# One long kernel, three places: who makes the high parts of a projection's weights, which column groups the first stage multiplies, and in which order latent attention begins

## The chip, the cores and the metric

The kernel runs on one core of one Trainium2 chip. The metric is the device time of one execution in microseconds, the median over several runs. A profiled execution gives the trace from which the rows below come.

## What is computed

The reference is two transformer blocks behind one another on x of 1024 tokens by 1024 features, batch 1, all in float32.

The first block normalizes x, makes six modulation vectors from one condition vector (`silu(c) @ w_ada + b_ada`, 1024 by 6144, split into shift, scale and gate twice), projects the modulated x by `w_in` into the inputs of a latent attention and of a retention mixer, mixes, projects back, and ends with a feed-forward part:

```python
mod = c_act @ w_ada[l] + b_ada[l]
sh1, sc1, gt1, sh2, sc2, gt2 = [m[:, None, :] for m in jnp.split(mod, 6, axis=-1)]
h = x * (1.0 + sc1) + sh1
proj = h @ w_in[l]
...
a = mla_mixer(...)            # 8 heads, causal, 64 plain + 32 rotated features per head
x = layer_norm(ALPHA * x + gt1 * y, ln1_g[l], ln1_b[l])
```

The second block has an "even" and an "odd" layer. The even layer projects 1024 features to 2560 (`e_w_in`), both for the 1024 tokens and for a context of 256, runs a depthwise convolution of 31 taps over 512 channels, and a Fourier mix over others.

## The kernel before

Activations lie with features on the 128 partitions: a tile is 128 features by 1024 tokens, eight tiles make a tensor (`X`, and `HH` and `HL` below). A large product is made of *units*: 128 output features for all tokens, accumulated in one PSUM tensor `G[s]` over eight feature tiles. To keep float32 accuracy with fast matrix products, activations and weights are both split into a rounded high part and the remainder: `HH` and `HL` for activations, `WH` and `WL` for weights; a unit is HH x WH, HL x WH and HH x WL (`gemm_unit`, line 304). For each unit SP loads a weight tile `RAW` (512 KB), POOL makes `WH` by a copy that rounds (line 266 or 278) and then `WL = RAW - WH` (line 269 or 281). Two buffers of each exist, so unit i can be split when unit i-2 has been multiplied (`unit_done`). Some engine then empties `G[s]` and increments `unit_freed`.

The program is a list of stages. In each, every engine has its own instruction list, and an engine enters a stage when ACT, PE and DVE have all left the one before (`gate`). POOL and SP run ahead, held only by their semaphores. TensorE alone may run the first unit of a following stage inside the one before (`lead_in`, the *lead unit*), as its activations appear.

- Stage `start`: SP loads x (eight DMAs) and then six column groups `ADA[g]` of `w_ada`, 512 columns each, 2 MB each: groups 0 and 1 are the shift, 2 and 3 the scale, 4 and 5 the gate of the first half. SP's queue then continues with the first weight tiles of `win`. TensorE multiplies groups 1 and 2 by the condition vector in products with one column (`ada`, line 506). DVE makes groups 0 and 3 by a multiplication (line 470) and a reduction (line 473), which TensorE sums over partitions (line 515). TensorE turns x (line 523), DVE writes tile f of `X` (line 481), ScalarE scales it with the modulation and makes `HH` (lines 420, 423), DVE makes `HL` (`h_low`, line 427). At the end TensorE multiplies groups 4 and 5.
- Stage `win`: 16 units of `w_in`. Beside it DVE makes the modulation vectors of the second half by rows (`Modulation`, block of 1024 columns: eight loads `WVEC` of 512 KB and eight multiply-adds, lines 374 and 377, then eight short sums on TensorE, line 393): three blocks. SP issues, at step j, the store of a tile of `X` to DRAM (6 <= j < 14), the weights of unit j, and two `WVEC` loads, in this order.
- Stage `mla` (latent attention): products of query and key parts (line 951, 959) and values (967); for the rows of a head's scores, eight maxima (`largest`, line 983, reduced by DVE, line 1245), which become a row of the query (`row`, `put_row`), then the steps of scores, exponential and values. The rotated 32 features are made by DVE (`rope_plain`, `rope_swapped`), rounded by ScalarE (`rope_high`, line 1126), completed by DVE (`rope_low`, line 1239) and put into the heads' tiles by SP's DMAs (line 1329).
- Stage `ein`: 20 units of `e_w_in`, each with the context's columns beside it (`side`, line 307). Units 0 to 7 feed the convolution, which DVE runs from SBUF to SBUF, tap by tap, for the 1024 tokens (`ACC`) and the 256 of the context (`ACCC`): four channel tiles of 31 taps, line 1945, in one streak of 88 taps from the moment unit 7 is done. At a change of channel tile there are two copies (line 1950) and two instructions with one input (line 1942). ScalarE empties the units 8 to 19. POOL splits all 20 by `split_unit`.

Of the kernel before, what the change touches and what calls it, by code (L numbers as in the profile page):

```python
# [14 lines left out]
F32 = mybir.dt.float32  # L15
# [7 lines left out]
P = 128  # L23
# [111 lines left out]
def build_program(nc, A, out):  # L135

    ctx = ExitStack()
    with ctx:
# [211 lines left out]
        class Modulation:  # L350
# [7 lines left out]

            def load(self, sp, q):
                g, (b, k) = self.first + q, divmod(q, KT)  # L360
                w, _, j, _, _ = self.blocks[b]
                need(sp, vec_used[g % 2], g // 2)
                sp.dma_start(self.raw[q % 2][:], A[w][k * P:(k + 1) * P, j * P:j * P + D]).then_inc(vec_loaded[g % 2], 16)

            def rows(self, dve, q):
                g, (b, k), raw = self.first + q, divmod(q, KT), self.raw[q % 2]
# [4 lines left out]
                for x, v in enumerate(xs):  # L371
                    acc = self.sums[b % 2][x][:]
                    if k == 0:
                        dve.tensor_scalar(acc, raw[:], v[:, 0:1], None, ALU.mult).then_inc(S("mod_row"), 1)
                    else:
                        dve.wait_ge(S("mod_row"), self.rows_done + 1 - len(xs))
                        dve.scalar_tensor_tensor(out=acc, in0=raw[:], scalar=v[:, k:k + 1], in1=acc, op0=ALU.mult,
# [7 lines left out]
            def sum(self, pe, b):  # L385
# [4 lines left out]
                for j in range(KT):  # L390
                    for x in range(len(xs)):
                        c = MOD_COL + j * len(xs) + x
                        m = pe.matmul(M[b % 2][:, c:c + 1], self.sums[b % 2][x][:, j * P:(j + 1) * P], ONES[:, 0:1],  # L393
                                      start=True, stop=True)
# [40 lines left out]
        ADA = [Z(f"ADA{g}", [P, KT, 512], F32, 64 + 16 * g if g < 4 else 32 + 16 * (g - 4)) for g in range(6)]  # L435

        def start_sp(sp, r0):
            for t in range(NT):
                sp.dma_start(XT[:, t, :], A["x"][t * P:(t + 1) * P, :]).then_inc(S("x_in"), 16)
            for g in range(6):  # L440
# [3 lines left out]
        def start_dve(dve):  # L444
# [20 lines left out]
            prod = X[:, 0:4, :].rearrange("p a (b n) -> p (a b) n", n=512)  # L465
            for i, g in enumerate((0, 3)):
                dve.wait_ge(S(f"ada{g}"), 16)
                if i:
                    dve.wait_ge(S("ada_rows"), 2)
                dve.tensor_tensor(prod, ADA[g][:], CACT[:].unsqueeze(2).broadcast_to([P, KT, 512]), ALU.mult)\  # L470
                   .then_inc(S("ada_rows"), 1)
                dve.wait_ge(S("ada_rows"), 2 * i + 1)
                dve.tensor_reduce(X[:, 4 + i, 0:512], prod.rearrange("p k n -> p n k"), AX.X, ALU.add)\
                   .then_inc(S("ada_rows"), 1)
# [4 lines left out]
            for f in range(KT):  # L479
                dve.wait_ge(S("li_tr"), f + 1)  # L480
                dve.tensor_scalar(X[:, f, :], M[f % 2][:], vec("ln_in_g", f), vec("ln_in_b", f), ALU.mult,
                                  ALU.add).then_inc(S("li_x"), 1)
                if f:
                    h_low(dve, "li", f - 1, SEQ)
            h_low(dve, "li", KT - 1, SEQ)
            dve.wait_ge(S("ada_sum"), 6)
            dve.tensor_tensor(MODA[:, 16:24], G[1][:, 0:8], vec("b_ada", 16, 8), ALU.add).then_inc(S("mod_in"), 1)
# [11 lines left out]
        def start_pe(pe):  # L499
            def ada(g):  # L500

                pe.wait_ge(S(f"ada{g}"), 16)
                for u in range(4):
                    col = 4 * (g % 4) + u
                    for k in range(KT):
                        m = pe.matmul(G[g // 4][:, col:col + 1], ADA[g][:, k, u * P:(u + 1) * P], CACT[:, k:k + 1],  # L506
                                      start=(k == 0), stop=(k == KT - 1))
                m.then_inc(S("ada_sum"), 1)
            pe.wait_ge(S("c_act"), 2)
            for g in (1, 2):  # L510
                ada(g)
            for i, g in enumerate((0, 3)):
                pe.wait_ge(S("ada_rows"), 2 * i + 2)
                for u in range(4):
# [2223 lines left out]
```

## Time and profile before

| what | value |
|---|---|
| median of 3 runs | 2986.7 us (2984.83 to 2994.78) |
| profiled execution | 2987.89 us |
| its span, first to last instruction | 2986.1 us |
| PE busy | 2587.2 us (87%) |
| DVE busy | 1375.1 us (46%) |
| POOL busy | 835.1 us (28%) |
| ACT busy | 569.2 us (19%) |

Busy time counts an instruction from its start to its end, including time in which it waits for a port inside. The shares are averages over stages that have different limits, so each edit has to be judged in its own stage. Of ends of TensorE's instructions the profile has only a model.

### The profile page before, as it was taken

How to read it: one execution, taken by the hardware profiler on the slowest of the kernel's cores; microseconds unless marked ns; L12 is line 12 of the kernel's file. 1: busy time of each engine (PE TensorE's matmuls, PEld its weight loads, DVE VectorE, ACT ScalarE, POOL GpSimd, SP SyncE). 2: the span in 40 equal slices, each digit the busy share in tenths (PEclk: the TensorE clock that was granted, in tenths of full speed). 3: DMA queues.
4: the chain of work that ended last, by engine and by line, in shares of the span. 5: the costliest groups of instructions: out<-in, count | busy, mean ns of one | idle time of the engine just before them, and what ended most of it. 6: DMA issues, size and time to landing. Idle time of an engine off the chain costs nothing.

```text
span 2986.1 us, 29208 instructions
## 1 busy us (share of the span) xinstructions
PE 2587.2 (87%) x11738; PEld 2026.1 (68%) x11738; DVE 1375.1 (46%) x1554; ACT 569.2 (19%) x818; POOL 835.1 (28%) x505
## 2 busy tenths in 40 slices
PE   5999668899999999999994994699498799959998
PEld 5887345567678888888762783575276588838877
DVE  7261753334643444444447689603523313046643
ACT  2001123440432101111125200000202300013310
POOL 1132230005463233223452358610021233210011
PEclk9799868999999999999997997899798899979999
DMA  7252000013132232222222100011211111140001
GB/s 259 92 169 64 18 16 0 15 57 96 56 102 85 88 99 89 78 88 85 80 86 92 36 28 16 28 32 44 86 52 33 36 49 42 42 104 16 1 15 71
DMA packets 219710, 190.12 MB, mean 64 GB/s; under 512 B 14928, under 2 KB 193744, under 8 KB 219344
## 3 DMA queue, kind: packets, MB, share of 16 engines
q1 hardware_dynamic: 214144, 167.93, 18.8%
q0 software_dynamic: 3872, 14.93, 1.3%
q10 hardware_dynamic: 1584, 5.77, 0.5%
q8 instruction: 72, 1.18, 0.2%
q14 instruction: 38, 0.31, 0.0%
HBM read 167.76 MB, written 13.63 MB: 61 GB/s over the span
## 4 chain that ended last, share of the span: by engine, by line
PE 72%; DVE 12%; issue 6%; ACT 4%; PEld 2%; DMA 1%; POOL 1%; PEldq 1%; SPq 1%; ACTq 0%; DVEq 0%; POOLq 0%
PE G L304 26%; PE G L1573 25%; PE M L2496 3%; PE M L307 2%; PE G L1029 2%; DVE WPT L2532 2%; PE M L2481 1%; PE M L1588 1%; PE M L393 1%; PE G L2060 1%; PE M L2060 1%; PEld G L506 1%; PE M L983 1%; PE M L951 1%; PE G L2191 1%
## 5 line engine op out<-in xcount | busy, mean ns | idle before, releaser
L304 PE MATMUL G<-HH,WH 128*128 128x512 f32 x1264 | 406.7, 402 | 118.7 <-POOL WL L269 71.9
L304 PE MATMUL G<-HL,WH 128*128 128x512 f32 x1264 | 401.2, 398 | 0.0
L304 PE MATMUL G<-HH,WL 128*128 128x512 f32 x1264 | 400.7, 397 | 0.0
L266 POOL TENSOR_SCALAR WH<-RAW 128x1024 fp32r<-128x1024 f32 x64 | 189.8, 2966 | 745.0 <-PE G L304 458.0
L278 POOL TENSOR_SCALAR WH<-RAW 128x1024 fp32r<-128x1024 f32 (+1 forms) x152 | 129.9, 855 | 929.0 <-PE G L1573 508.8
L304 PEld LDWEIGHTS G<-HH,WH 128*128 128x128 f32 x1264 | 224.6, 191 | 174.3 <-issue 115.7
L281 POOL TENSOR_TENSOR WL<-RAW,WH 128x1024 fp32r<-128x1024 f32 (+1 forms) x152 | 294.4, 1937 | 12.7
L304 PEld LDWEIGHTS G<-HL,WH 128*128 128x128 f32 x1264 | 225.6, 191 | 47.3
L304 PEld LDWEIGHTS G<-HH,WL 128*128 128x128 f32 x1264 | 225.4, 191 | 47.5
L1573 PE MATMUL G<-HH,WH 128*128 128x512 f32 x640 | 228.4, 405 | 14.2 <-POOL WL L281 9.5
L1573 PE MATMUL G<-HL,WH 128*128 128x512 f32 x640 | 225.0, 400 | 0.0
L1573 PE MATMUL G<-HH,WL 128*128 128x512 f32 x640 | 224.9, 400 | 0.0
L1704 DVE SCALAR_TENSOR_TENSOR X<-G,MODA,X 128x512 f32<-128x512 f32 (+1 forms) x96 | 97.4, 1015 | 206.5 <-PE G L1573 206.2
L1573 PE MATMUL G<-FHT,WH 128*128 128x512 f32 x512 | 177.1, 407 | 8.9 <-issue 5.3
L1720 DVE TENSOR_TENSOR FLT<-T,FHT 128x1024 fp32r<-128x1024 f32 (+1 forms) x40 | 53.3, 1332 | 278.9 <-ACT FHT L1661 278.9
L1573 PE MATMUL G<-FLT,WH 128*128 128x512 f32 x512 | 174.5, 402 | 0.0
L1573 PE MATMUL G<-FHT,WL 128*128 128x512 f32 x512 | 173.7, 400 | 0.0
L1945 DVE SCALAR_TENSOR_TENSOR ACC<-U,V,ACC 128x1024 f32<-128x1024 f32 x120 | 162.5, 1354 | 0.7 <-DVE UC L1965 0.7
L269 POOL TENSOR_TENSOR WL<-RAW,WH 128x1024 fp32r<-128x1024 f32 x64 | 160.0, 2500 | 5.3
L1573 PEld LDWEIGHTS G<-HH,WH 128*128 128x128 f32 x640 | 122.1, 191 | 48.1 <-issue 11.9
L1657 ACT ACTIVATE T<-G 128x1024 f32<-128x1024 f32 (+1 forms) x40 | 34.2, 855 | 604.3 <-PE G L1573 604.3
L1573 PEld LDWEIGHTS G<-HL,WH 128*128 128x128 f32 x640 | 121.8, 190 | 31.0 <-issue 1.7
(467 smaller groups left out, 4097.7 us busy)
## 6 DMA issues: line engine op xcount, KB each, us to landing
RAW<-in_w_ff SPq DMA_DIRECT2D x40, 512.0 KB, 4.0
RAW<-in_w_ff SPq DMA_DIRECT2D x80, 256.0 KB, 2.8
ADA<-in_w_ada SPq DMA_DIRECT2D x6, 2048.0 KB, 19.7
WVEC<-in_w_ada SPq DMA_DIRECT2D x24, 512.0 KB, 4.5
FVEC<-in_e_w_mod SPq DMA_DIRECT2D x24, 512.0 KB, 4.0
FVEC<-in_o_w_mod SPq DMA_DIRECT2D x24, 512.0 KB, 3.9
RAW<-in_o_w_in SPq DMA_DIRECT2D x24, 512.0 KB, 3.7
RAW<-in_e_w_in SPq DMA_DIRECT2D x20, 512.0 KB, 3.7
```

The lines of the kernel that those rows point to most:

```text
L266: pool.tensor_scalar(WH[s][:], RAW[s][:], 1.0, 0.0, ALU.mult, ALU.add).then_inc(w_high, 1)
L269: pool.tensor_tensor(WL[s][:], RAW[s][:], WH[s][:].bitcast(F32), ALU.subtract).then_inc(w_split[s], 1)
L278: pool.tensor_scalar(hi, raw, 1.0, 0.0, ALU.mult, ALU.add).then_inc(w_high, 1)
L281: pool.tensor_tensor(lo, raw, hi.bitcast(F32), ALU.subtract).then_inc(w_split[U % 2], 1)
L304: m = pe.matmul(G[s][:, n * w:(n + 1) * w], part[s][:, k, :], acts[i][:, k, n * w:(n + 1) * w], start=first, stop=last)
L307: m = pe.matmul(M[s][:, 0:CTX], part[s][:, k, :], side[i][:, k, :], start=first, stop=last)
L1029: pe.matmul(G[1][:, cols_], VP[:, kb_, first:first + P], PF[g % 4][:, 0:n], start=(kb_ == 0), stop=(kb_ == 4 * c + 3)).then_inc(S("ml_pv"), 1)
L1573: m = pe.matmul(G[s][:, half(h)], part[s][:, k, :], moving[:, half(h)], start=(j == 0 and part is WH and moving is hi), stop=(j == len(ord ...
L1704: dve.scalar_tensor_tensor(out=X[:, f, cc], in0=G[U % 2][:, cc], scalar=gate, in1=X[:, f, cc], op0=ALU.mult, op1=ALU.add).then_inc(unit_fr ...
L1945: dve.scalar_tensor_tensor(out=acc[:], in0=u[:, j, k:k + T], scalar=wk, in1=acc[:], op0=ALU.mult, op1=ALU.add).then_inc(tap, 1)
L2060: m = pe.matmul(dst, vv[:, tt, g * P:(g + 1) * P], tab[:, q * half:(q + 1) * half], start=(i == 0 and q == 0), stop=(q == 1 and (t >= NT o ...
L2496: m = pe.matmul(M[1][:, c0:c0 + HEAD], WPT[i % 2][:, b * P:(b + 1) * P], v, start=(b == 0), stop=(b == len(blocks) + 1))
```

## The change

1. In stage `ein`, `WH` of units 2 to 19 is made by ScalarE (`ein_high`), after it has emptied unit i-2; POOL has its own program there, waits for ScalarE's copy and makes only `WL`. Units 0 and 1 are split as before.
2. In stage `start`, groups 4 and 5 are neither loaded nor multiplied. Group 1 alone is multiplied by TensorE; groups 2 and 3 are made by DVE by rows (one multiplication and seven multiply-adds of 512 columns each), group 0 by POOL by rows (eight multiplications and seven additions). TensorE turns two tiles ahead of the sums, and DVE writes these two tiles of `X` before it adds up the modulation. The gate is a fourth block of `Modulation` in `win`, with buffers in `X`, whose tiles are therefore stored from step 2 on.
3. In stage `mla`, ScalarE rounds the rotated part of the first query pair first; its high parts go out by two DMAs with a semaphore of their own, and the first maxima wait for these alone. `v_part(0)` moves behind the first maximum, the maxima of head 0 alternate between two PSUM tensors, `scores(0)` comes after the fifth of them and `row(0, 0)` after the first two scores. ScalarE loads the exponential's table at the stage's begin. POOL makes the key rows of heads 1 to 3 only after DVE's `rope_low(0)`.

```diff
-        ADA = [Z(f"ADA{g}", [P, KT, 512], F32, 64 + 16 * g if g < 4 else 32 + 16 * (g - 4)) for g in range(6)]
+        ADA = [Z(f"ADA{g}", [P, KT, 512], F32, 64 + 16 * g) for g in range(4)]
+        ROWS = {g: X[:, 4 + i, 0:512] for i, g in enumerate((2, 3, 0))}
...
-            for i, g in enumerate((0, 3)):
+            for i, g in enumerate((2, 3)):
                 dve.wait_ge(S(f"ada{g}"), 16)
...
+                dve.tensor_scalar(ROWS[g], ADA[g][:, 0, :], CACT[:, 0:1], None, ALU.mult).then_inc(S("ada_rows"), 1)
+                for k in range(1, KT):
+                    dve.wait_ge(S("ada_rows"), KT * i + k)
+                    dve.scalar_tensor_tensor(out=ROWS[g], in0=ADA[g][:, k, :], scalar=CACT[:, k:k + 1], in1=ROWS[g],
+                                             op0=ALU.mult, op1=ALU.add).then_inc(S("ada_rows"), 1)
...
+        def start_pool(pool):
+            part = X[:, 7, 0:512]
+            pool.wait_ge(S("c_act"), 2)
+            pool.wait_ge(S("ada0"), 16)
+            pool.tensor_scalar(ROWS[0], ADA[0][:, 0, :], CACT[:, 0:1], None, ALU.mult).then_inc(S("ada_pool"), 1)
+            for k in range(1, KT):
+                pool.wait_ge(S("ada_pool"), 2 * k - 1)
+                pool.tensor_scalar(part, ADA[0][:, k, :], CACT[:, k:k + 1], None, ALU.mult).then_inc(S("ada_pool"), 1)
+                pool.wait_ge(S("ada_pool"), 2 * k)
+                pool.tensor_tensor(ROWS[0], ROWS[0], part, ALU.add).then_inc(S("ada_pool"), 1)
...
+            pe.wait_ge(S("li_xn"), NT)
+            for f in range(2):
+                turn(f)
+            pe.wait_ge(S("ada_pool"), 2 * KT - 1)
+            sums(0)
+            for i, g in enumerate((2, 3)):
+                pe.wait_ge(S("ada_rows"), KT * i + KT)
+                sums(g)
+            for f in range(2, KT):
+                turn(f)
...
-        WMOD = Modulation([ada_block(j) for j in (24, 32, 40)], [Z("WVEC0", [P, D], F32, 72), Z("WVEC1", [P, D], F32, 60)],
-                          [[Z("WSUM0", [P, D], F32, 56)], [Z("WSUM1", [P, D], F32, 52)]])
+        WMOD = Modulation([ada_block(j) for j in (24, 32, 40, 16)],
+                          [Z("WVEC0", [P, D], F32, 72)[:], Z("WVEC1", [P, D], F32, 60)[:], X[:, 1, :], X[:, 2, :]],
+                          [[Z("WSUM0", [P, D], F32, 56)[:]], [Z("WSUM1", [P, D], F32, 52)[:]], None, [X[:, 0, :]]])
...
+            WMOD.sum(pe, 3)
...
-                if 6 <= j < 14:
-                    sp.dma_start(SPILL[:, j - 6, :], X[:, j - 6, :]).then_inc(x_spilled, 16)
+                if 2 <= j < 10:
+                    sp.dma_start(SPILL[:, j - 2, :], X[:, j - 2, :]).then_inc(x_spilled, 16)
                 if j >= 4:
                     load_unit(sp, (r0 + j) // 2, j % 2, win_unit(j), RAW[j % 2][:])
-                if j < 12:
-                    WMOD.load(sp, 2 * j)
-                    WMOD.load(sp, 2 * j + 1)
+                if j == 12:
+                    sp.wait_ge(x_spilled, 16 * KT)
+                WMOD.load(sp, 2 * j)
+                WMOD.load(sp, 2 * j + 1)
...
-                need(pe, S("ml_mx"), 8 * h + n)
+                ps = M[0]
+                if h == 0:
+                    need(pe, S("ml_mx"), n - 1)
+                    if n % 2:
+                        pe.wait_ge(S("ml_qlo"), 2)
+                        ps = G[0][:, 512:] if n > 4 else G[0]
+                else:
+                    need(pe, S("ml_mx"), 8 * h + n)
...
-            v_part(0)
             pe.wait_ge(S("ml_rot"), 2)
             for n in range(NT):
                 largest(0, n)
+                if n == 0:
+                    v_part(0)
                 if n == 4:
                     row(0, 1)
-            row(0, 0)
-            scores(0)
+                    scores(0)
...
+            act.wait_ge(mla_split, N_SPLIT)
+            act.activation(PF[0][0:1, 0:32], IDENT[0:1, 0:32], ACT.Exp)
+            rope_high(0)
             q_high(0)
             k_high(0)
-            rope_high(0)
...
+            sp.wait_ge(S("ml_qrh"), 1)
+            for odd in range(2):
+                put(0, odd, 0, S("ml_rope_first"))
+            sp.wait_ge(S("ml_qr"), 1)
+            for odd in range(2):
+                put(0, odd, 1, S("ml_rope_in0"))
...
+        def ein_high(act, i):
+
+            r, U_ = info("ein")["r0"] + i, info("ein")["u0"] + i
+            if 2 <= i < 20:
+                act.wait_ge(raw_loaded[r % 2], (r // 2) * 16 + 16)
+                act.wait_ge(unit_done[U_ % 2], U_ // 2)
+                act.activation(WH[U_ % 2][:], RAW[r % 2][:], ACT.Copy).then_inc(ein_wh, 1)
+
+        def ein_pool(pool):
...
+                if i < 2:
+                    split_one(pool, r, U_, KT)
+                    continue
+                pool.wait_ge(ein_wh, i - 1)
+                pool.sem_inc(w_high, 1)
+                pool.wait_ge(w_split[U_ % 2], U_ // 2)
+                pool.tensor_tensor(WL[U_ % 2][:], RAW[r % 2][:], WH[U_ % 2][:].bitcast(F32), ALU.subtract)\
+                    .then_inc(w_split[U_ % 2], 1)
```

## Rows read from the trace of the kernel before

**Rows 1.** Stretches: length, busy us (instructions) by engine, PE clock, DMA share, GB/s.

```profile
75.00:102.00 27.00, 27.00 (x128) 27.00 (x128) 5.30 (x5) 4.93 (x5) 0.00 (x0) 0.50 0.00 1
...
116.00:290.00 174.00, 173.33 (x767) 140.09 (x768) 73.19 (x72) 4.36 (x4) 53.76 (x28) 1.00 0.45 136
...
1826.00:1862.00 36.00, 13.48 (x71) 11.22 (x69) 35.90 (x47) 3.48 (x5) 35.92 (x2) 0.76 0.00 0
```

**Rows 2.** Timeline of PE, first stage: start us, us, line, names, [idle before]

```profile
25.59 27.44 PE L506 MATMUL G<-CACT,ADA 128*128 128x1 f32 x128 [25.59 <-DMA ADA<-in_w_ada]
...
52.89 1.85 PE L515 MATMUL G<-ONES,X 128*128 128x1 f32 x8
...
57.42 6.26 PE L523 MATMUL M<-IDENT,XT 128*128 128x128 f32 x32
...
116.08 0.71 PE L304 MATMUL G<-HH,WH 128*128 128x512 f32 x2 [0.36 <-PEq L2638]
```

**Rows 3.** Timeline of DVE, first stage

```profile
26.53 5.88 DVE L462 TENSOR_SCALAR XT<-XT,MV,RS 128x1024 f32<-128x1024 f32 x8
...
32.31 4.42 DVE L470 TENSOR_TENSOR X<-ADA,CACT 128x4096 f32<-128x4096 f32 x1
...
59.41 1.34 DVE L481 TENSOR_SCALAR X<-M,V 128x1024 f32<-128x1024 f32 x1 [1.43 <-PE M L523]
```

**Rows 4.** Timeline of ACT, first stage

```profile
60.85 1.24 ACT L420 ACTIVATE T<-X,MODA 128x1024 f32<-128x1024 f32 x1 [34.59 <-DVE X L481]
...
62.13 1.06 ACT L423 ACTIVATE HH<-T 128x1024 fp32r<-128x1024 f32 x1
```

**Rows 5.** Timeline of DVE, stage win

```profile
128.89 3.41 DVE L377 SCALAR_TENSOR_TENSOR WSUM<-WVEC,CACT,WSUM 128x1024 f32<-128x1024 f32 x1 [1.61 <-DMA WVEC<-in_w_ada]
...
133.58 1.28 DVE L377 SCALAR_TENSOR_TENSOR WSUM<-WVEC,CACT,WSUM 128x1024 f32<-128x1024 f32 x1
...
167.08 2.14 DVE L564 SCALAR_TENSOR_TENSOR ANGR<-TURN,ANGR 128x512 f32<-128x512 f32 x3
```

**Rows 6.** Timeline of POOL, stage win

```profile
128.82 2.40 POOL L281 TENSOR_TENSOR WL<-RAW,WH 128x1024 fp32r<-128x1024 f32 x1
```

**Rows 7.** Timeline of POOL, stage ein

```profile
1661.96 1.05 POOL L266 TENSOR_SCALAR WH<-RAW 128x1024 fp32r<-128x1024 f32 x1 [17.62 <-PE M L307]
...
1690.40 8.90 POOL L266 TENSOR_SCALAR WH<-RAW 128x1024 fp32r<-128x1024 f32 x1 [10.39 <-PE M L307]
...
1718.24 9.52 POOL L266 TENSOR_SCALAR WH<-RAW 128x1024 fp32r<-128x1024 f32 x1 [10.39 <-PE M L307]
...
1773.92 32.60 POOL L266 TENSOR_SCALAR WH<-RAW 128x1024 fp32r<-128x1024 f32 x1 [10.38 <-PE M L307]
...
1809.58 1.93 POOL L266 TENSOR_SCALAR WH<-RAW 128x1024 fp32r<-128x1024 f32 x1 [0.32 <-POOL WL L269]
...
1880.78 36.24 POOL L266 TENSOR_SCALAR WH<-RAW 128x1024 fp32r<-128x1024 f32 x1 [11.52 <-PE M L307]
```

**Rows 8.** Timeline of DVE, stage ein

```profile
1761.65 2.97 DVE L1945 SCALAR_TENSOR_TENSOR ACC<-U,V,ACC 128x1024 f32<-128x1024 f32 x1 [0.24 <-DVE UC L1965]
...
1772.90 1.28 DVE L1945 SCALAR_TENSOR_TENSOR ACC<-U,V,ACC 128x1024 f32<-128x1024 f32 x1
...
1774.49 1.28 DVE L1945 SCALAR_TENSOR_TENSOR ACC<-U,V,ACC 128x1024 f32<-128x1024 f32 x1
...
1810.53 1.25 DVE L1945 SCALAR_TENSOR_TENSOR ACCC<-UC,V,ACCC 128x256 f32<-128x256 f32 x1
```

**Rows 9.** Chain that ended last, latent attention's begin

```profile
437.82 0.95 ACT QRH L1126
...
444.62 1.19 PE M L983 x2
...
463.57 3.77 PE M L951 x12
```

**Rows 10.** Chain that ended last, in stage win

```profile
161.12 1.68 PE M L393 x16
```

More of the change, by code:

```diff
@@ L357, in __init__, with raw_of, sums_of @@
                 vec_count[0] += KT * len(blocks)
+            def raw_of(self, q):
+                return self.raw[q % 2 + (2 if len(self.raw) == 4 and q >= 3 * KT else 0)]
+            def sums_of(self, b):
+                return self.sums[b if b < len(self.sums) and self.sums[b] else b % 2]
             def load(self, sp, q):
@@ L392, in sum @@
                         c = MOD_COL + j * len(xs) + x
[L393 removed]
+                        m = pe.matmul(M[b % 2][:, c:c + 1], self.sums_of(b)[x][:, j * P:(j + 1) * P], ONES[:, 0:1],
                                       start=True, stop=True)
@@ L439, in start_sp @@
                 sp.dma_start(XT[:, t, :], A["x"][t * P:(t + 1) * P, :]).then_inc(S("x_in"), 16)
-            for g in range(6):
+            for g in range(4):
                 sp.dma_start(ADA[g][:], A["w_ada"][:, 512 * g:512 * g + 512].rearrange("(k p) n -> p k n", p=P))\
@@ L499, in start_pe, with sums, turn @@
         def start_pe(pe):
-            def ada(g):
-                pe.wait_ge(S(f"ada{g}"), 16)
+            def sums(g):
                 for u in range(4):
[L504 to L514, printed above, removed]
-                    m = pe.matmul(G[0][:, 4 * g + u:4 * g + u + 1], X[:, 4 + i, u * P:(u + 1) * P], ONES[:, 0:1],
+                    m = pe.matmul(G[0][:, 4 * g + u:4 * g + u + 1], ROWS[g][:, u * P:(u + 1) * P], ONES[:, 0:1],
                                   start=True, stop=True)
                 m.then_inc(S("ada_sum"), 1)
-            pe.wait_ge(S("li_xn"), NT)
-            for f in range(KT):
+            def turn(f):
                 if f >= 2:
@@ L573, in win_dve @@
             for j in range(16):
+                for q in (2 * j, 2 * j + 1):
+                    WMOD.rows(dve, q)
                 if j < 12:
-                    for q in (2 * j, 2 * j + 1):
-                        WMOD.rows(dve, q)
                     unit_ready(dve, u0 + j)
@@ L1046, in extras @@
                     if i == 0:
+                        row(0, 0)
+                    if i == 1:
                         take()
@@ L1093, in mla_pe, with rope_rows @@
             spread(N_PAIR - 1)
+        def rope_rows(pe, h, high):
+            j = h // 2
+            if j == 0:
+                pe.wait_ge(*((S("ml_rope_first"), 32) if high else (S("ml_rope_in0"), 32)))
+            else:
+                pe.wait_ge(S(f"ml_rope_in{j % 2}"), (0, 64, 96, 128)[j])
         def ROW_AT(h):
@@ L1171, in extras @@
                     chunk(h - 1, 0)
+                if h == 0 and i == 0:
+                    put_row(0, 0)
                 if h == 0 and i == 4:
@@ L1972, in ein_dve @@
             conv(dve, step, 4 * CONV_W)
+        ein_wh = whole("ein_high")
+        def ein_high(act, i):
[5 more added lines that the diff above has]
+        def ein_pool(pool):
+            r0, u0 = info("ein")["r0"], info("ein")["u0"]
+            for i in range(20):
+                r, U_ = r0 + i, u0 + i
+                if i < 2:
[6 more added lines that the diff above has]
+                    .then_inc(w_split[U_ % 2], 1)
+                pool.wait_ge(w_split[U_ % 2], U_ // 2 + 1)
+                pool.sem_inc(raw_used[r % 2], 1)
         def ein_act(act):
@@ L1995, in ein_act @@
                 act.sem_inc(unit_freed[U_ % 2], 1)
+                ein_high(act, 10 + j)
         def ein_src(j):
             return A["e_w_in"][:, ein_cols[j]:ein_cols[j] + P].rearrange("(k p) n -> p k n", p=P)
-        stage("ein", dict(lead=lead_in("ein", SEQ, "en_lo", side=(HHC, HLC)), act=ein_act, dve=ein_dve,
+        stage("ein", dict(lead=lead_in("ein", SEQ, "en_lo", side=(HHC, HLC)), act=ein_act, dve=ein_dve, pool=ein_pool,
                           pe=lambda pe: gemm_pairs(pe, info("ein")["u0"], 10, SEQ, (HH, HL), led=True, side=(HHC, HLC))),
```

94 lines of the change are left out of this document (51 added, 43 removed).

## The prediction

> **What bounds the kernel now.** I began with the granted clock and busy time by stretch, because a share of the span hides that the three edited places have different limits. Four stretches matter [rows 1]. From 75 to 102 us TensorE does 128 instructions for gate columns and nothing else, at half clock, with every other engine nearly idle: it is the bound. From 116 to 290 TensorE is busy 173.3 of 174 us: that stage (`win`) hides whatever DVE, POOL and the queues do, so long as its weights arrive. From 1826 to 1862 TensorE is busy 13.5 of 36 us, while POOL is "busy" 35.9 in two instructions: POOL is the bound, and behind POOL something else. The timelines of the engines then say what.
>
> In the first stage, TensorE makes the products of column groups 1 and 2 from 25.59 to 53.0, sums DVE's rows for groups 0 and 3, and turns tiles; after the last turn it makes groups 4 and 5, and only then, at 102, starts the lead unit of `win`, which lasts until 115.7 (the next unit's first row, 116.08, less its 0.36 of idle time), when `win` proper begins [rows 1, 2]. DVE scales x from 26.53 to 32.3 and works on rows for groups 0 and 3 from 32.31 until about 55.6, the turns of 57.42 less the last sum's 1.85 [rows 2, 3]. ScalarE's first tile of h begins at 60.85, 1.24 for the scaled tile and 1.06 for its high part, so one tile per 2.3 us [rows 4].
>
> In `ein` a POOL copy WH<-RAW, 1.05 us at 1661.96, takes 8.9, 9.5 and then three times over 32 us (first and last of the three in [rows 7]). Its starts show the pace of a unit: 1690.40 to 1718.24 is two units, so 13.92 us each. DVE meanwhile runs the convolution, a tap of x and a tap of the context every 1.59 us, each instruction starting before the one ahead has ended [rows 8]. POOL gets in only when DVE pauses or changes channel. Once in, it gets in again: at 1809.58 the next copy waits for one DVE instruction (1.93 us), and then DVE is the one that is stretched (1.25 us for a 256-column tap) [rows 7, 8].
>
> **Start, products of the gate removed.** Groups 4 and 5 cost 27.0 us on the path [rows 1]. They go to `win` as eight more DVE rows and 8 column sums.
>
> **Start, products of groups 0, 2, 3 by rows.** TensorE keeps group 1 alone: its data lands at 25.59, half of the 27.4 us is 13.7, so it ends at 39.3. Two turns (the 32 transposes took 6.26, so about 1.6 to 1.9 each) end at 43.0, three sums of 1.85 at 48.6 [rows 2]. On DVE, a 512-column multiply-add is 2.14/3 = 0.71 us with its wait [rows 5]; two groups are 2 x (0.45 + 7 x 0.71) = 10.9 us, instead of 23.3. From 32.3 [rows 3] that ends at R = 43.5 if nothing disturbs it (R is when DVE's rows are done). POOL's group 0 is 8 multiplications and 7 additions of 512 columns; at half the 1.05 of a copy [rows 7] and half the 2.4 of a subtraction [rows 6], with some 0.1 us between, 8 x 0.63 + 7 x 1.3 = 14 us, from about 20 us (group 0 lies 2 MB ahead of group 1 in the same queue, which moves about 370 GB/s there).
>
> But POOL and DVE exclude each other: a DVE multiply-add that started at 128.89 beside POOL's subtraction of 128.82 took 3.41 us instead of 1.28: it ended 1.1 us after POOL's, which had taken 2.40 [rows 5, 6]. They do not share, one waits for all of the other. About 7 us of POOL's row work lie after 26.5, and the splits of units 0 and 1 (two times 1.05 + 2.4 = 6.9 us), whose loads come 4 MB earlier than before, fall near 39. If all of this pushes DVE, R is 43.5 + 13.5 = 57.0. I take R = 54, near the exclusive end, since the row shows full exclusion, less some overlap with waits. Two tiles of x (1.34 each) follow R [rows 3], so the scale of h is ready at R + 2.7 = 56.7.
>
> From there to the end of the lead unit: turn 7 needs tile 5 of x, about 10 us after h begins, then 2 for the turn, then 13.7 for the unit, which starts at half clock as it did before, 102 to 115.7 [rows 1, 2]: 26 us in all. h itself comes at 2.3 per tile [rows 4], ahead of that. End 56.7 + 26 = 82.7 against 115.7: **-33**. Bounds: R = 43.5 (then the sums, 48.6, decide) ends at 74.6, -41; R = 57 ends at 85.7, -30.
>
> **`win`.** DVE's eight rows more, 1.28 us each [rows 5], find room: it works 73 of 174 us [rows 1]. Eight more loads of 0.5 MB pass SP, and the stores of X start at j = 2 instead of 6, ahead of the load of unit 4 with three stores instead of none. At 136 GB/s with 0.45 of the engines busy a full queue moves about 300 GB/s [rows 1], 1.7 us a store, so unit 4's weights can be 0 to 5 us late; there was some 3 us of room. I take 1. The fourth sum comes after the last unit: 1.68 us on TensorE [rows 10], less the 1.0 that ScalarE needs for its last tile anyway, plus two short DVE instructions behind it: 1. **+2**, bounds 0 and +5. SP's wait for all stores at j = 12 costs nothing: the last store is issued at j = 9.
>
> **Latent attention's begin.** Before, ScalarE copied the high parts of q and k until 437.82, then rounded the rotated part (0.95); DVE's low part, four of SP's DMAs and their landing followed, and the first maximum began at 444.62 [rows 9]. After, ScalarE rounds first, and only two DMAs of high parts stand before the maximum, in flight while q and k are copied. What is last is then the copy of k: 437.82 + 0.95 = 438.8 if everything on ScalarE moves back by the rounding. So -5.8 there. POOL's other key rows wait, so they no longer lie over DVE's addition. v_part (24 short products on TensorE) moves behind the first maximum, where DVE reduces; with two buffers the maxima overlap. Eight maxima, one behind the other, took from 444.62 to some 459, and DVE's eight reductions are 6 us of that; with TensorE's half under them I estimate 438.8 + 13.4 = 452.2 for scores(1) and 457.3 for q_part, one more step (1.3 us) then being done ahead of it, against 463.57 [rows 9]: 463.57 - 457.3 + 1.3 = 7.6, **-7.5**. Lower bound on the gain 4 (the begin alone, minus clock that falls in a new pause), upper 10. The exponential's table load leaves a place where it was covered; nothing.
>
> **`ein`, WH by ScalarE.** Removed from POOL: 18 copies. ScalarE gains 18 x 1.06 us [rows 4] in a stage where it is idle for 12 us of each 13.92; it makes WH(i) after it emptied unit i-2, 1.5 us later than POOL did, and TensorE has a unit's time for it. No cost. The question is who waits for DVE now. The subtraction WL stays on POOL and reads SBUF too; it is now POOL's *first* instruction after ten idle microseconds, in the place of the copy. The trace has no subtraction in that place: each follows its copy by 0.1 us. Its wait is between nothing and what the copy waited. The nearest rows are the copies, which never got in in mid-streak after idling (five of the six that came then, the sixth waited 1.3 us for a change of channel [rows 7]) and the one exclusion of a subtraction [rows 5, 6]; so I take the same wait. Then each channel change still lets through two units, and the gain is the copy and its intrusion into DVE, two changes of channel at 1 to 1.5 us and the last 1.05: **-4**, bounds -2 and -8.
>
> SBUF — State Buffer, section "Who interferes with whom", of the Trainium skill says that the second to issue is blocked until the first finishes. By that rule a copy waits at most 1.3 us; the 32.60 us in [rows 7] disagree, so the rule holds for one pair and not for a streak. Were it to hold for the subtraction, `ein` would lose its stalls: rival 1.
>
> Sum: -33 + 2 - 7.5 - 4 = -42.5 on the profiled execution's 2987.9 (span 2986.1, 1.8 around it) gives 2945.4; the median of the runs shown is 1.2 lower, so 2944.
>
> **Rivals.** (1) The subtraction gets in between two taps, as it does after its copy. TensorE then runs through: the lead unit ends at 1661.9, so unit 14 starts 13 x 13.92 later, at 1842.9. It started when the copy of 1880.78 and its subtraction were done, at 1919.5: 76.6 later, and each stall also cost about 1 us of half clock. DVE takes 88 taps of 1.59 from 1761.7, 4 us of copies and 11 subtractions of 2.4, to 1932 [rows 7, 8], 6 us past TensorE's last unit (1661.9 + 19 x 13.92 = 1926). So -74 in place of -4: 2874. For it: after 1809.58 this happens, and the subtraction is another program on POOL. Against: the copies that waited. (2) It gets in at some places (a pause of the streak that now falls elsewhere): each of three stalls is worth some 22 to 25 us: 2895 to 2920. (3) The first stage gives less: POOL's row for group 0 is starved by DVE's eight scalings in a row (5.88 us [rows 3]) and by its rows, so the sum of group 0 comes last, R at 62: -25, total 2952 to 2960. (4) The other side: `win` becomes load-bound. Loads of weights stand behind two rows and a store on SP, and if they lag each unit from 4 to 15 by over 3.5 us, 12 x 3.5 = 42 us eat the whole gain; 5 us each would give 3004. Against: TensorE waited under 1 of 174 us, and the extra stores only move. (5) No net change, by half of that.
>
> **Chances.** Forecast 0.58 (its own range, bounds of the four terms added: -59 to -31, so 2928 to 2956); rival 1 0.20; rival 2 0.10; rival 3 0.07; rival 4 0.03; rival 5 0.02. The range reaches from rival 1 with a margin of 5 to the forecast's slow end: 2868 to 2957. 0.3% is 9 us, about what a measurement here tells from no change: faster 0.95, same 0.02, slower 0.03.
>
> **What would show it.** After: `win` proper begins near 83 us; DVE rows of 512 end near 54 and some are stretched to about 1.9 us; TensorE in `win` is busy all but 2 us. The first maximum of head 0 comes 16 us after TensorE's first product of the stage, not 22. In `ein`, WL rows of 30 us and more stand where WH rows stood, three times, with TensorE at 13.5 busy in 36. The prediction is wrong if those WL rows are 2.4 to 3.7 us long, if R is past 60, or if TensorE waits for unit 4.

## The result, and the profile after

| kernel | median of runs | profiled run |
|---|---|---|
| before, beside it | 2986.47 us (2984.83 to 2994.78, 4 runs) | 2987.89 us |
| changed | 2941.27 us (2934.71 to 2952.76, 4 runs) | 2934.71 us |

The ratio is 0.9847, 95% interval 0.9812 to 0.9883: 45 us faster, in the middle of the forecast's range and 3 us from its number. The profiled run of the changed kernel is the fastest of its four, so its trace shows 53 us. The kernel before has a median of 2979.38 us in 23 runs told below, 7 us less than in the four beside the changed kernel, so the gain may well be nearer to 37 than to 45 us. Of all runs told below, one execution of the last version (4267.05 us, mean granted clock 0.553 where its others had 0.943) is left out of its ratio.

Where the 53 us lie, by the starts of the same instructions in both traces:

| stretch | before | changed | difference |
|---|---|---|---|
| start of the program to the end of the lead unit of `win` | 115.7 | 83.8 | -31.9 |
| `win` | 175.9 | 177.6 | +1.7 |
| retention's products ahead of latent attention (code unchanged) | 73.9 | 66.5 | -7.4 |
| latent attention's first product to its first maximum | 22.0 | 16.0 | -6.0 |
| from there to its last division | 225.8 | 224.7 | -1.1 |
| output projection and feed-forward (unchanged) | 946.9 | 942.5 | -4.4 |
| `ein`, from the end of unit 8 to the last unit emptied | 232.5 | 228.7 | -3.8 |
| all the rest (unchanged) | | | about -0.3 |

The four edited places make 41 us; the forecast's terms for them were -33, +2, -7.5 and -4, which is -42.5. The other 12 us come from code that is the same, and some 3.5 us of the first row are not the edit's either, but the clock's (see the account of the start below).

Windows of the changed kernel (columns as in [rows 1]):

```profile
70.00:72.00 2.00, 1.43 (x7) 1.04 (x6) 2.00 (x3) 1.97 (x3) 0.00 (x0) 0.50 0.00 0
72.00:74.00 2.00, 2.00 (x12) 1.73 (x11) 2.00 (x3) 1.97 (x3) 0.00 (x0) 0.95 0.00 0
...
84.00:255.00 171.00, 169.72 (x750) 136.90 (x751) 83.60 (x79) 4.37 (x4) 54.15 (x28) 1.00 0.53 163
1774.00:1812.00 38.00, 14.03 (x73) 11.68 (x72) 37.90 (x47) 6.00 (x7) 35.07 (x1) 0.74 0.00 0
```

`win` is as full as before: TensorE waits 1.3 of 171 us, with the DMA share at 0.53 in place of 0.45. The last line is the stall of [rows 1] again: TensorE busy 14 of 38 us, POOL "busy" 35 in one instruction.

First stage, timeline of PE, then of DVE, then of POOL, of the changed kernel:

```profile
26.26 13.79 PE L536 MATMUL G<-CACT,ADA 128*128 128x1 f32 x64 [26.26 <-DMA ADA<-in_w_ada]
39.91 3.65 PE L530 MATMUL M<-IDENT,XT 128*128 128x128 f32 x16
46.70 3.58 PE L522 MATMUL G<-ONES,X 128*128 128x1 f32 x16 [3.14 <-POOL X L507]
58.51 1.86 PE L522 MATMUL G<-ONES,X 128*128 128x1 f32 x8 [8.24 <-DVE X L479]
...
72.39 0.71 PE L304 MATMUL G<-HH,WH 128*128 128x512 f32 x2
...
84.20 0.70 PE L304 MATMUL G<-HH,WH 128*128 128x512 f32 x2 [0.36 <-PEq L2727]
```

```profile
27.18 10.49 DVE L471 TENSOR_SCALAR XT<-XT,MV,RS 128x1024 f32<-128x1024 f32 x8
37.59 0.82 DVE L476 TENSOR_SCALAR X<-ADA,CACT 128x512 f32<-128x512 f32 x1
38.45 8.74 DVE L479 SCALAR_TENSOR_TENSOR X<-ADA,CACT,X 128x512 f32<-128x512 f32 x7
...
48.41 10.05 DVE L479 SCALAR_TENSOR_TENSOR X<-ADA,CACT,X 128x512 f32<-128x512 f32 x7
58.38 2.59 DVE L484 TENSOR_SCALAR X<-M,V 128x1024 f32<-128x1024 f32 x2
```

```profile
20.89 1.57 POOL L502 TENSOR_SCALAR X<-ADA,CACT 128x512 f32<-128x512 f32 x1 [17.82 <-DMA ADA<-in_w_ada]
...
45.16 1.49 POOL L507 TENSOR_TENSOR X<-X 128x512 f32<-128x512 f32 x1
46.62 1.48 POOL L278 TENSOR_SCALAR WH<-RAW 128x1024 fp32r<-128x1024 f32 x1
...
52.12 2.65 POOL L281 TENSOR_TENSOR WL<-RAW,WH 128x1024 fp32r<-128x1024 f32 x1
```

TensorE's third sum waits for DVE (8.24 us of idle time), so DVE's rows are what comes last. They end at R = 58.46. While POOL works, eight scalings take 10.49 us (5.88 in [rows 3]) and seven multiply-adds 8.74 and 10.05. The lead unit runs from 72.39 to 83.8, 11.5 us: the granted clock was 0.50 (1.2 GHz) only from 68.8 to 72.2 us, under the last turns, and back at its upper level (2.4 GHz) with the unit's first products.

Latent attention's begin, timeline of PE, and of ScalarE, changed kernel:

```profile
400.50 1.19 PE L1018 MATMUL M<-KHT,QHT 96*128 96x512 f32 x2 [3.79 <-ACT KHT L1150]
...
401.58 5.36 PE L994 MATMUL M<-WVV,KVS 128*128 128x128 f32 x24
```

```profile
395.18 1.06 ACT L1174 ACTIVATE QRH<-QROT 128x1024 fp32r<-128x1024 f32 x1 [9.26 <-DVE QROT L1287]
396.15 2.05 ACT L1150 ACTIVATE QHT<-G 64x1024 fp32r<-64x1024 f32 x2
398.22 2.06 ACT L1150 ACTIVATE KHT<-G 64x1024 fp32r<-64x1024 f32 x2
```

Rounding comes first, the copies of q and k hide the two DMAs, the maximum waits for k's copy alone.

`ein`, timeline of POOL, changed kernel:

```profile
1699.06 2.41 POOL L2055 TENSOR_TENSOR WL<-RAW,WH 128x1024 fp32r<-128x1024 f32 x1 [12.93 <-ACT WH L2043]
...
1726.96 31.29 POOL L2055 TENSOR_TENSOR WL<-RAW,WH 128x1024 fp32r<-128x1024 f32 x1 [12.98 <-ACT WH L2043]
1758.52 2.51 POOL L2055 TENSOR_TENSOR WL<-RAW,WH 128x1024 fp32r<-128x1024 f32 x1 [0.27 <-POOL WL L2055]
1776.86 35.07 POOL L2055 TENSOR_TENSOR WL<-RAW,WH 128x1024 fp32r<-128x1024 f32 x1 [15.83 <-ACT WH L2043]
1812.21 2.51 POOL L2055 TENSOR_TENSOR WL<-RAW,WH 128x1024 fp32r<-128x1024 f32 x1 [0.28 <-POOL WL L2055]
1830.98 34.65 POOL L2055 TENSOR_TENSOR WL<-RAW,WH 128x1024 fp32r<-128x1024 f32 x1 [16.26 <-ACT WH L2043]
```

Three subtractions of 31 to 35 us stand where three copies stood [rows 7], each followed by one that gets in at once.

### The profile page after: what moved, and what is told of

Read it like the earlier page. It is cut to its first block, busy times and chain, and to the rows that moved or that the text cites. A ratio compares the mean times of both kernels' runs of the same rounds, so it can differ in the third digit from the quotient of the medians.

```text
span 2932.9 us, 28884 instructions
## 1 busy us (share of the span) xinstructions
PE 2538.7 (87%) x11570; PEld 1980.0 (68%) x11570; DVE 1384.4 (47%) x1574; ACT 588.2 (20%) x837; POOL 825.4 (28%) x502
## 4 chain that ended last, share of the span: by engine, by line
PE 73%; DVE 12%; POOL 4%; ACT 4%; issue 3%; PEld 1%; DMA 1%; PEldq 1%; SPq 1%; ACTq 0%; DVEq 0%; POOLq 0%
PE G L304 26%; PE G L1634 25%; POOL WL L2055 3%; PE M L2585 3%; PE M L307 2%; PE G L1067 2%; DVE WPT L2621 2%; PE M L2570 1%; PE M L1649 1%; PE M L400 1%; PE G L2149 1%; PE M L2149 1%; PE M L978 1%; PE G L2280 1%; DVE HL L434 1%
## 5 line engine op out<-in xcount | busy, mean ns | idle before, releaser
L278 POOL TENSOR_SCALAR WH<-RAW 128x1024 fp32r<-128x1024 f32 (+1 forms) x154 | 136.1, 884 | 846.0 <-PE G L1634 501.6
L1634 PE MATMUL G<-HH,WH 128*128 128x512 f32 x640 | 227.6, 404 | 13.8 <-POOL WL L281 9.1
L266 POOL TENSOR_SCALAR WH<-RAW 128x1024 fp32r<-128x1024 f32 x44 | 46.6, 1060 | 593.0 <-PE G L304 457.2
L2055 POOL TENSOR_TENSOR WL<-RAW,WH 128x1024 fp32r<-128x1024 f32 x18 | 148.4, 8247 | 186.0 <-ACT WH L2043 185.2
```

Source lines behind the costliest of these rows:

```text
L278: pool.tensor_scalar(hi, raw, 1.0, 0.0, ALU.mult, ALU.add).then_inc(w_high, 1)
L1634: m = pe.matmul(G[s][:, half(h)], part[s][:, k, :], moving[:, half(h)], start=(j == 0 and part is WH and moving is hi), stop=(j == len(ord ...
L2055: pool.tensor_tensor(WL[U_ % 2][:], RAW[r % 2][:], WH[U_ % 2][:].bitcast(F32), ALU.subtract)\
```

## The experiments

**The parts one by one.** Each is the kernel before with one numbered part of the change, and one run is the changed kernel again, all on one chip (before there: 2979.38 us, 2968.33 to 2995.28, 23 runs).

Part 1 alone:

```diff
+                ein_high(act, 2 * j + 2)
+                ein_high(act, 2 * j + 3)
...
-        stage("ein", dict(lead=lead_in("ein", SEQ, "en_lo", side=(HHC, HLC)), act=ein_act, dve=ein_dve,
+        stage("ein", dict(lead=lead_in("ein", SEQ, "en_lo", side=(HHC, HLC)), act=ein_act, dve=ein_dve, pool=ein_pool,
```

> The kernel before with part 1 alone (WH of the even projection by ScalarE). Theory (the subtraction waits as the copy did): -4 us, 2982 to 2984, three WL of 31 to 36 us in the stage ein. Rival (the subtraction gets in between two taps): -70 or more, 2915, no WL above 4 us. In the trace of the changed kernel the stage ended 3.9 us earlier against its begin, but nothing there separates it from the clock.

2976.35 us (12 runs), ratio 1.0 (0.9979 to 1.0021): not told from no change. In the trace the stretch of `ein` is 227.8 us instead of 232.5, -4.7, and the three long waits are subtractions.

Part 2 alone:

```diff
-            for i, g in enumerate((0, 3)):
+            for i, g in enumerate((2, 3)):
...
+        def start_pool(pool):
...
-        WMOD = Modulation([ada_block(j) for j in (24, 32, 40)], [Z("WVEC0", [P, D], F32, 72), Z("WVEC1", [P, D], F32, 60)],
+        WMOD = Modulation([ada_block(j) for j in (24, 32, 40, 16)],
```

> The kernel before with part 2 alone (first stage without the gate's products, gate in win). Theory: the lead unit of win ends near 84 instead of 115.7 and win gives back 2: -30 us, 2956. Rival (part 2 also earned the 7 us by which the retention stage was shorter after, through something it moves): -37, 2949, and the retention stage shorter in every execution of it.

2946.62 us (6 runs), ratio 0.9895 (0.9869 to 0.9921), -33. The rival (that the shorter retention stretch belongs to this part) falls: that stretch is 66.3 us here, but also 66.3 and 66.5 in the runs of parts 1 and 3, whose first stage is the old one.

Part 3 alone:

```diff
+            rope_high(0)
             q_high(0)
             k_high(0)
-            rope_high(0)
...
+                if n == 0:
+                    v_part(0)
```

> The kernel before with part 3 alone (latent attention's begin). Theory: -7 us, 2979 to 2980, first maximum 16 us after the first product of the stage. Rival (the gain is lost again by the clock, which falls in the new pauses): 0 to -3.

2972.77 us (11 runs), ratio 0.9974 (0.9956 to 0.9992), -6.6; first product to first maximum 16.0 us, to the end 224.7, as in the whole change.

The changed kernel once more:

> The changed kernel once more. Theory of the clock: its profile differs from the one on record by several us in stages that the change does not touch (the retention stage 0 or 7 us longer, the feed-forward stage by 1.6 us steps), and the median comes out at 2941 to 2946, the sum of the three parts (-41 to -42). Rival: the 12 us in untouched stages belong to the change; then the profile repeats the one on record within 1 us per stage and the median is below 2938.

2942.29 us (4 runs), ratio 0.9884 (0.9858 to 0.9910), -37. The three parts add up to -42.4; the two measurements of the whole gave -45 and -37. Of the 8 us between these two, 7.1 lie in the kernel before (2986.47 and 2979.38) and 1.0 in the changed one. The sum and both measurements agree within their intervals, so no part is seen to work through another; with intervals of 8 us each way, an effect of a few us would not show. The retention stretch is 66.7 us in this profile too, so the theory's case of 7 us more did not come up.

**The wait of POOL in the convolution.** Prediction and change left the largest loss of `ein` in place, so it was tried next, on the changed kernel: one more wait for DVE on its own previous instruction, the context's tap. It orders nothing that was not in order already; it only makes the next tap of x start after the tap before it has ended.

```diff
                     if q:
                         dve.wait_ge(tap, q)
+                    if i == 0 and q:
+                        dve.wait_ge(S("ein_ctap"), q)
```

> The changed kernel, and in the convolution every tap of x also waits for the context's tap just ahead of it, so that DVE stops for a moment once per tap. Theory (POOL never gets in while DVE's instructions follow one another without a pause): WL enters at the next pause, no WL above 4 us, TensorE runs through, the stage ein about 70 us shorter, DVE's convolution its bound: 2870 to 2885. Rival (whatever DVE does, a POOL instruction after long idle time loses to two-input instructions): WL still 30 us and more, time 2941 to 2955.

2872.29 us (5 runs), ratio 0.9640 (0.9626 to 0.9655; before on this chip 2978.95 us, 11 runs). All subtractions take 2.4 to 3.5 us, and `ein` from the end of unit 8 to the last unit emptied is 154.9 us instead of 228.7. The price: a pair of taps every 1.79 us instead of 1.59, so the convolution ends 14 us after ScalarE has emptied the last unit. Hence the same at every eighth tap only:

```diff
+                    if i == 0 and q and q % 8 == 0:
+                        dve.wait_ge(S("ein_ctap"), q)
```

> As gap_each, but the additional wait stands at every eighth tap only. Theory: WL waits up to 8 taps, 13 us at most, mean 6 us; TensorE has 13.9 us per unit less 1.5 for ScalarE's emptying, 1.06 for its copy and 2.4 for WL, so about 9 us of wait are covered: nearly as fast as gap_each, within 10 us of it. Rival: as there, no gain.

2868.00 us (5 runs), ratio 0.9626 (0.9605 to 0.9648); the convolution now ends with the last unit. A window of this kernel, then POOL's timeline, then DVE's:

```profile
1774.00:1812.00 38.00, 38.00 (x199) 32.33 (x198) 37.69 (x39) 8.37 (x10) 9.16 (x3) 1.00 0.13 39
```

```profile
1736.58 8.47 POOL L2057 TENSOR_TENSOR WL<-RAW,WH 128x1024 fp32r<-128x1024 f32 x1 [12.98 <-ACT WH L2045]
1750.44 2.74 POOL L2057 TENSOR_TENSOR WL<-RAW,WH 128x1024 fp32r<-128x1024 f32 x1 [5.39 <-ACT WH L2045]
1764.37 2.69 POOL L2057 TENSOR_TENSOR WL<-RAW,WH 128x1024 fp32r<-128x1024 f32 x1 [11.19 <-ACT WH L2045]
```

```profile
1759.35 0.48 DVE L2008 SCALAR_TENSOR_TENSOR ACCC<-UC,V,ACCC 128x256 f32<-128x256 f32 x1
1759.93 1.28 DVE L2008 SCALAR_TENSOR_TENSOR ACC<-U,V,ACC 128x1024 f32<-128x1024 f32 x1
...
1764.32 0.47 DVE L2008 SCALAR_TENSOR_TENSOR ACCC<-UC,V,ACCC 128x256 f32<-128x256 f32 x1
1764.72 3.42 DVE L2008 SCALAR_TENSOR_TENSOR ACC<-U,V,ACC 128x1024 f32<-128x1024 f32 x1
```

TensorE is busy 38 of 38 us, at full clock. The pause is the 0.10 us between 1759.83 (1759.35 + 0.48) and 1759.93. But the subtraction of 1764.37 got in with no pause beside it: the next tap, 1764.72, is the one that waited (3.42 us). The one of 1736.58 had to wait 6 us, for the pause at 1742.8. What differs is the distance from the last pause.

**Does it need ScalarE's copies?** The kernel before, with the wait at every eighth tap alone:

```diff
+                    if i == 0 and q and q % 8 == 0:
+                        dve.wait_ge(S("ein_ctap"), q)
```

> The kernel before, with the one added wait of the experiment gap_8 in its convolution (every eighth tap of x also waits for the context's tap ahead of it); GpSimd still makes both parts of each weight tile. Theory (the pause is what lets GpSimd in, whoever makes the high parts): the copies WH<-RAW fall from over 30 us to under 9, TensorE waits for splits no longer, and the stage from its first split to its last unit's copy out is some 75 us shorter, as in gap_8: 2978 - 75 = 2903. Rival (the pause only works with ScalarE's copies, because a copy and a subtraction are two entries between taps and the copy is the harder one): at least two copies stay above 20 us and the time is 2925 or more.

2906.86 us (5 runs), ratio 0.9754 (0.9729 to 0.9779), -75, expected 2903; before on this chip 2981.51 us. POOL's timeline:

```profile
1786.23 1.85 POOL L266 TENSOR_SCALAR WH<-RAW 128x1024 fp32r<-128x1024 f32 x1 [9.89 <-PE M L307]
1788.16 2.46 POOL L269 TENSOR_TENSOR WL<-RAW,WH 128x1024 fp32r<-128x1024 f32 x1
...
1828.23 6.32 POOL L266 TENSOR_SCALAR WH<-RAW 128x1024 fp32r<-128x1024 f32 x1 [6.03 <-PE M L307]
```

The longest copy is 6.32 us and `ein` again 154.9: this one wait does nearly all, part 1 is not needed for it. Part 1 gets a use of its own only then: without it the convolution takes 162.3 us from the end of unit 8 on, with it (gap_8) 154.2, since DVE has ten copies fewer to let in there; it is the last to end.

**Distance of the pauses.** In twelve traces up to here, each GpSimd instruction that came while taps were running was set against the number of taps of x begun since DVE's last pause (a gap of 0.1 us, a channel change, a wait for a unit). Up to four: it waited 1.3 us or less. Five and more: until the next pause. The number of taps divides them better than the time does: in gap_8 the subtraction of 1750.44 came four taps, but 7.5 us, after a pause and waited 0.3 us, while that of 1736.58 came five taps and only 6.6 us after one and waited 6.1. Two runs to test this, as gap_8 with 4 and with 16 in the place of 8:

```diff
-                    if i == 0 and q and q % 8 == 0:
+                    if i == 0 and q and q % 4 == 0:
                         dve.wait_ge(S("ein_ctap"), q)
```

> The changed kernel with the added wait in the convolution at every fourth tap of x instead of every eighth. In the traces so far every GpSimd instruction that arrived at most four taps of x after the last pause in VectorE's streak (a gap between two of its instructions, however short) waited 1.3 us or less, also without a pause beside it, and those that arrived five to twelve taps after it waited for the next pause. If the number of taps since the last pause decides, no subtraction of the stage is over 3.8 us here (2.4 plus at most 1.3), where gap_8 still had four of 5.3 to 8.5. TensorE did not wait for those four, so the time is that of gap_8, 2868 plus or minus 8. Rival (what counts is that a pause happens to fall where GpSimd arrives): waits stay spread up to the distance of the pauses, 4 x 1.6 = 6.4 us, so subtractions of up to 8.8 us.

> The same with the added wait at every sixteenth tap of x (pauses also at the changes of channel, every 31 taps). By the taps since the last pause: subtractions that arrive within four taps of one take 2.4 to 3.7 us, those that arrive later take what is left to the next pause, up to 11 x 1.6 = 18 us and 2.4 more; GpSimd has some 11 us of room in each unit, so TensorE waits for the longest ones, by up to 9 us each, and the stage is 5 to 30 us longer than in gap_8, 2873 to 2898. No subtraction lasts over 21 us. Rival (one pause early in the streak is enough, what locks GpSimd out is something that builds up only over twenty taps and more): all under 4 us and the time of gap_8.

pause_4: 2865.54 us (4 runs), ratio 0.9620 (0.9573 to 0.9667), longest subtraction 3.54 us. pause_16: 2866.45 us (4 runs), ratio 0.9623 (0.9576 to 0.9670). POOL's timeline of pause_16:

```profile
1769.81 3.23 POOL L2057 TENSOR_TENSOR WL<-RAW,WH 128x1024 fp32r<-128x1024 f32 x1 [6.06 <-ACT WH L2045]
1783.73 12.52 POOL L2057 TENSOR_TENSOR WL<-RAW,WH 128x1024 fp32r<-128x1024 f32 x1 [10.69 <-ACT WH L2045]
1797.65 2.40 POOL L2057 TENSOR_TENSOR WL<-RAW,WH 128x1024 fp32r<-128x1024 f32 x1 [1.40 <-ACT WH L2045]
...
1841.16 15.03 POOL L2057 TENSOR_TENSOR WL<-RAW,WH 128x1024 fp32r<-128x1024 f32 x1 [11.35 <-ACT WH L2045]
```

These four came 3, 10, 2 and 9 taps after a pause. The second waited 10.1 us with the next pause 10.4 away, the fourth 12.6 with it 12.9 away. Over all fourteen traces: 104 instructions within four taps, longest wait 1.15 us; 65 beyond, every one waited until the streak's next break. The rivals of both runs fall. The time of pause_16 was missed: the stretch of `ein` is 161.5 us, 7.5 longer than in gap_8, inside the 5 to 30 us expected, but the median (2873 to 2898 expected) is that of gap_8. A difference of 7.5 us is within these intervals of 14 us each way, so this run doesn't show what the longer waits cost in all.

**The first stage.** DVE's rows came last, so POOL's work was taken from under them: first the splits of units 0 and 1, on the changed kernel.

```diff
                 pool.tensor_tensor(ROWS[0], ROWS[0], part, ALU.add).then_inc(S("ada_pool"), 1)
+            pool.wait_ge(S("ada_rows"), 2 * KT)
```

> The changed kernel, and POOL begins to split the weights of units 0 and 1 of win only when DVE's rows of groups 2 and 3 are done. Theory (POOL and DVE exclude each other, each us of POOL under DVE's rows costs DVE one): rows done at 51 to 52 instead of 58.5, the lead unit ends at 77 instead of 83.9, time -7. Rival (DVE's rows are slow for another reason, their data or their chain): rows still at 58, time 0.

2939.14 us (6 runs), ratio 0.9871 (0.9849 to 0.9893): no difference from the changed kernel that these runs can tell, where 7 us were expected. Then also POOL's rows of group 0 (the first half of the shift is left out, zeros stand in its place):

```diff
-            pool.tensor_scalar(ROWS[0], ADA[0][:, 0, :], CACT[:, 0:1], None, ALU.mult).then_inc(S("ada_pool"), 1)
...
-                pool.tensor_tensor(ROWS[0], ROWS[0], part, ALU.add).then_inc(S("ada_pool"), 1)
+            pool.memset(ROWS[0], 0.0).then_inc(S("ada_pool"), 2 * KT - 1)
```

> late_split with POOL's row for group 0 replaced by a memset: eight multiplications and seven additions are left out, and half of the shift is wrong by it. Theory of exclusion: DVE's eight scalings take 5.9 us again, not 10.5, and its rows 11 us; rows done at 44 to 45, the sums (48.6) then decide, lead unit ends near 75. Rival: scalings and rows as slow as in the changed kernel.

2938.57 us in a single run, whose profile has 7.3 us more in the retention stretch and 6.8 more in the feed-forward than the changed kernel's, so only its first stage is read here. DVE's timeline of late_split, then of no_pool_rows:

```profile
38.59 8.75 DVE L479 SCALAR_TENSOR_TENSOR X<-ADA,CACT,X 128x512 f32<-128x512 f32 x7
47.27 0.47 DVE L476 TENSOR_SCALAR X<-ADA,CACT 128x512 f32<-128x512 f32 x1
47.78 5.47 DVE L479 SCALAR_TENSOR_TENSOR X<-ADA,CACT,X 128x512 f32<-128x512 f32 x7
```

```profile
26.93 5.87 DVE L471 TENSOR_SCALAR XT<-XT,MV,RS 128x1024 f32<-128x1024 f32 x8
...
39.15 5.47 DVE L479 SCALAR_TENSOR_TENSOR X<-ADA,CACT,X 128x512 f32<-128x512 f32 x7
```

R (the end of DVE's rows) falls from 58.46 to 53.25 without the splits (51 to 52 expected) and to 44.6 without POOL's rows too. The lead unit ends at 81.1 (77 expected) and 73.0 instead of 83.8. So the splits push DVE by 5.2 us, the rows by 8.6, of which 4.6 in the scalings. Of the 5.2 only 2.7 arrive, because the moved splits now lie over DVE's next work. Timeline of POOL, then of DVE, late_split:

```profile
54.48 2.36 POOL L281 TENSOR_TENSOR WL<-RAW,WH 128x1024 fp32r<-128x1024 f32 x1
...
58.16 2.36 POOL L281 TENSOR_TENSOR WL<-RAW,WH 128x1024 fp32r<-128x1024 f32 x1
```

```profile
55.87 0.98 DVE L491 TENSOR_SCALAR MODA<-MODA 128x8 f32<-128x8 f32 x1
...
59.26 2.34 DVE L434 TENSOR_TENSOR HL<-T,HH 128x1024 fp32r<-128x1024 f32 x1 [0.90 <-ACT HH L430]
```

In the changed kernel these two DVE instructions took 0.17 and 1.23 us: 1.9 of the 2.5 us that do not arrive. About 0.6 is left for the clock (0.50 from 63.3 to 70.1 us here, from 68.8 to 72.2 in the changed kernel), with a lead unit of 11.8 us instead of 11.5.

**Both edits together** (wait at every eighth tap, splits late):

> The changed kernel with both edits: the added wait of gap_8 in the convolution and, as in late_split, GpSimd's first two weight splits only after DVE's modulation rows. If the two places are independent the gains add: lead unit done near 81.5 us instead of 84.6, 2866 to 2868 as a median, at most 3 us under gap_8. Rival: the later splits delay the first units and the time is that of gap_8 or above.

2855.49 us (median of five; 2853.16 to 2856.76), ratio 0.9574 (0.9553 to 0.9594): 126 us under before on this chip, the best version. That is 12.5 us below gap_8 (on another chip), where 3 were expected: in the two profiles 3.7 us are the first stage, as expected, but 7.5 are the retention stretch (66.3 us against 73.8 in gap_8's profile) and 3.4 the feed-forward, both unchanged code. There the clock was at its lower level for 39 us in gap_8 and 21 in this one (retention), and for 58 and 48 us (feed-forward).

## Why the prediction was right, point by point

**Start, -33 (measured -31.9): right in sum, by errors against each other, and so in part luck.** R was taken as 54, with 57 as the end for full exclusion (its two terms, 7 and 6.9 us, add up to 13.9 and not to the 13.5 used); it was 58.46. Undisturbed, DVE's rows end at 44.6 (no_pool_rows; forecast 43.5, a multiply-add with its wait being 0.78 and not 0.71), so POOL's work added 13.8 us. That this equals the exclusive sum is a coincidence of two wrong steps. The first is the price of POOL's rows: 14 us, some 7 of them beside DVE's work, where they took 25.8 (20.89 to 46.65), 19.4 of them beside it. The multiplication of 512 columns takes 1.57 us beside DVE's statistics of x, which keep their 1.23 us, where half a copy made 0.63. The second is full exclusion: from 27.2 us on POOL was busy 26.3 us with rows and splits, or 22.3 at the durations that it has without DVE's rows beside it (an estimate from its rows), while DVE lost 13.8.

Behind R, the forecast had 28.7 us (2.7 + 26) and 25.4 were needed, 2.2 of it because the lead unit ran 11.5 us and not 13.7. "Starts at half clock as it did before" was carried over from a stretch in which TensorE had worked at half clock for 27 us [rows 1]; here turns at upper clock lay ahead. In after_again the clock came back only at 75.5 us, and the unit took 13.0. In the three other traces with the old start the lead unit was done at 111.8 to 112.3 and not at 115.7: the clock rose at 102.3 to 102.8 us, where the profile of before had 107.1. Against these traces the edit is worth 27 to 29 us. Rival 3, POOL's row starved, had the right ingredient (the scalings) with the roles changed: DVE was slowed, and the sum of group 0 was not last.

**`win`, +2 (+1.7): right.** The stores that come earlier cost nothing that shows; TensorE idles 1.3 us in 171. Rival 4, load-bound, did not happen at a DMA share of 0.53.

**Latent attention, -7.5 (-7.1; alone -6.6): right.** The begin gave 6.0 of the 5.8 forecast, through the very chain named; the overlap of the maxima gave 1.1 where 1.7 was left. That 1.1 isn't shown to be the edit's: from first maximum to last division the four traces with the old code have 221.3 to 227.5 us, those with the new one 223.3 to 225.1.

**`ein`, -4 (-3.8; alone -4.7 in the trace, median -3.0 with an interval that holds zero): right.** The choice "I take the same wait" carried the forecast. It came out right, but its reason, a comparison of copies with subtractions, is not what decides. The fourteen traces show that the kind of instruction does not matter: copies and subtractions alike get in within four taps of a pause. The three long subtractions of the changed kernel came nine taps or more after one. What the forecast called "once in, it gets in again" is that rule. Rival 1 rested on the same observation and had the wrong condition; its price was good: it said 2874 for a subtraction that gets in, and the kernels in which it does run in 2866 to 2872.

SBUF — State Buffer, section "Who interferes with whom", of the Trainium skill has the second engine blocked until the first finishes. For one pair this case agrees (a wait of at most 1.15 us behind a tap of 1.27, 104 times); behind five taps or more in a row it does not, with waits of up to 35.6 us.

**What the sum did not hold.** 12 us of the profile's 53 are stages with the same code. The retention stretch takes 66.2 to 66.7 us in eleven of the traces and 73.8 or 73.9 in three others (before, gap_8, no_pool_rows). In the middle of it the granted clock was 0.50 for 27 us in before (380.1 to 407.5) and for 7 us in the changed kernel (362.3 to 369.2); the whole stretch has 39 us at the lower level in the three long traces and 18 to 21 in the eleven short ones. The feed-forward stretch follows the clock too: 940 us with 48 or 51 us at the lower level, 942 to 944 with 58, 945 to 947 with 65, 949 with 72. What sets which of them one gets is open.

## What to carry to other kernels

When one engine runs a long streak of SBUF instructions that overlap by some hundredths of a microsecond, another engine may be locked out for the whole streak; look for its rows of tens of microseconds, and put a dependent wait every four to eight instruction pairs before moving its work to a third engine. Removing work from the engine that waits is worth only that work (here 4 us), removing the wait was worth 75. And compare an edit by the stage it touches, in several traces of each kernel: unchanged stages moved by 7 us with the clock.

## What the hardware did that was not expected

- The lock-out has a sharp edge: within four x-taps (eight instructions) of DVE's last pause POOL got in after at most 1.15 us, from the fifth on it never did before the next break (104 and 65 cases). It goes by the number of taps and not by the time since the pause: four taps and 7.5 us got in, five taps and 6.6 us did not. A pause of 0.1 us is enough. Why the edge lies at four was not found.
- DVE's scalings with one tensor input went from 5.88 to 10.49 us for eight beside POOL's rows, and POOL's multiplications from 1.57 to 2.01: both were slowed, neither was locked out.
- POOL's multiplication of 128 x 512 by a column took 1.57 us, more than its rounding copy of 128 x 1024 (1.05 us).
